# A third seven-product square in the last pair of an FFN block, and squares that wait for their parts one by one

## The reference

```python
def channel_mixer(h, up, conv_w, conv_b, down):
    hid = causal_dwconv(h @ up, conv_w, conv_b)      # 2048 -> 2 x 4096, convolution over 3 tokens
    gate, val = jnp.split(hid, 2, axis=-1)
    return (jax.nn.gelu(gate, approximate=True) * val) @ down   # 4096 -> 2048
```

## Time and profile before

| | |
|---|---|
| median of 3 runs | 3218.95 us (3218.23 to 3219.16) |
| the profiled execution's own time | 3219.05 us |
| its span in the trace | 3217.3 us |
| PE matmul busy | 3204.4 us, 100% of the span, 16261 matmuls |
| PE weight load busy | 2718.8 us, 85% |
| DVE busy | 2315.8 us, 72% |
| ACT busy | 1714.7 us, 53% |
| POOL busy | 183.0 us, 6% |
| chain that ended last | PE 99% of the span |
| DMA | 611.01 MB, mean 190 GB/s |
| granted TensorE clock | 0.999 in the mean |

### The profile page before, as it was taken

One profiled execution on the slowest core, in us unless ns is written; L12 is line 12 of the kernel. 1 busy time (PEld: TensorE's weight loads), 2 busy tenths in 40 slices (PEclk: granted clock), 3 DMA queues, 4 the chain that ended last, 5 costly groups with the idle time before them and its releaser, 6 DMA issues.

```text
span 3217.3 us, 42163 instructions
## 1 busy us (share of the span) xinstructions
PE 3204.4 (100%) x16261; PEld 2718.8 (85%) x16261; DVE 2315.8 (72%) x3007; ACT 1714.7 (53%) x2407; POOL 183.0 (6%) x194
## 2 busy tenths in 40 slices
PE   9999999999999999999999999999999999999999
PEld 7888888888888888888988888888888888888887
DVE  6576568767686877777565677877786667787777
ACT  6555545454554545455454565555565746555454
POOL 1033100010000000001000200000010020000001
PEclk9999999999999999999999999999999999999999
DMA  8945666665666666666656556666666545666665
GB/s 266 255 128 158 177 185 198 202 216 187 184 195 197 193 194 189 202 187 192 199 166 190 170 179 189 187 200 189 185 202 192 179 156 179 188 193 198 187 189 173
DMA packets 325452, 611.01 MB, mean 190 GB/s; under 512 B 19708, under 2 KB 47176, under 8 KB 324640
## 3 DMA queue, kind: packets, MB, share of 16 engines
q1 hardware_dynamic: 321776, 596.15, 60.9%
q0 software_dynamic: 3504, 12.52, 1.5%
HBM read 605.32 MB, written 3.28 MB: 189 GB/s over the span
## 4 chain that ended last, share of the span: by engine, by line
PE 99%; DMA 0%; ACT 0%; SPq 0%; DVE 0%; issue 0%; DVEq 0%; ACTq 0%
PE ps L546 21%; PE ps L387 16%; PE ps L389 16%; PE ps L388 16%; PE ps L549 11%; PE ps L398 2%; PE ps L400 2%; PE ps L399 2%; PE ps L534 2%; PE ps L532 2%; PE ps L533 2%; PE ps L726 1%; PE ps L750 1%; PE ps L621 1%; DMA raw<-w_in 0%; PE ps L715 0%
## 5 line engine op out<-in xcount | busy, mean ns | idle before, releaser
L373 DVE TENSOR_TENSOR w_lo<-raw,w_hi 128x1024 fp32r<-128x1024 f32 (+3 forms) x1041 | 1244.9, 1236 | 355.0 <-ACT w_hi L362 335.9
L362 ACT ACTIVATE w_hi<-raw 128x1024 fp32r<-128x1024 f32 (+3 forms) x1041 | 1041.4, 1039 | 395.5 <-DMA raw<-ffn_up 79.6
L546 PE MATMUL ps<-l_both,w_hi 128*128 128x512 f32 x2944 | 934.0, 396 | 0.0
L549 PEld LDWEIGHTS ps<-l_both,w_lo 128*128 128x128 f32 x2944 | 553.2, 188 | 122.4
L549 PE MATMUL ps<-l_both,w_lo 128*128 128x256 f32 x2944 | 594.4, 278 | 0.0
L546 PEld LDWEIGHTS ps<-l_both,w_hi 128*128 128x128 f32 x2944 | 456.1, 189 | 8.8
L387 PE MATMUL ps<-w_hi,m_hi 128*128 128x512 f32 (+1 forms) x1180 | 457.2, 387 | 0.0
L389 PE MATMUL ps<-w_hi,m_lo 128*128 128x512 f32 (+1 forms) x1180 | 454.6, 385 | 0.0
L388 PE MATMUL ps<-w_lo,m_hi 128*128 128x512 f32 (+1 forms) x1180 | 454.0, 385 | 0.0
L387 PE MATMUL ps<-w_hi,l_both 128*128 128x512 f32 (+3 forms) x1168 | 447.6, 383 | 0.7 <-DVE l_both L648 0.7
L389 PE MATMUL ps<-w_hi,l_both 128*128 128x512 f32 (+3 forms) x1168 | 440.4, 377 | 0.0
(11 more groups left out here) (633 smaller groups left out, 3499.1 us busy)
## 6 DMA issues: line engine op xcount, KB each, us to landing
raw<-ffn_up SPq DMA_DIRECT2D x256, 512.0 KB, 3.7
raw<-w_in SPq DMA_DIRECT2D x175, 512.0 KB, 3.7
raw<-w_mlp_in SPq DMA_DIRECT2D x128, 512.0 KB, 3.8
raw<-w_mlp_out SPq DMA_DIRECT2D x128, 512.0 KB, 4.3
raw<-ffn_down SPq DMA_DIRECT2D x128, 512.0 KB, 4.1
raw<-ab_w_in SPq DMA_DIRECT2D x64, 512.0 KB, 3.6
raw<-w_branch SPq DMA_DIRECT2D x48, 512.0 KB, 3.9
raw<-cd_w_in SPq DMA_DIRECT2D x40, 512.0 KB, 3.9
```

The costliest lines, as they stand in the source:

```text
L362: nc.scalar.activation(w_hi[:, k % RING, 0:n], raw[:, k % RING, 0:n], ACT.Copy).then_inc(hi_done, 1)
L373: nc.vector.tensor_tensor(w_lo[:, k % RING, 0:n], raw[:, k % RING, 0:n], w_hi[:, k % RING, 0:n].bitcast(F32), ALU.subtract).then_inc(lo_do ...
L546: return nc.tensor.matmul(ps[:, banks[t], :], hi[:, j, P * t:P * (t + 1)], l_both[:, kt, :], start=opens, stop=stop)
L549: return nc.tensor.matmul(ps[:, banks[t], 0:TOK], lo[:, j, P * t:P * (t + 1)], lh[0][:, kt, :], start=False, stop=stop)
```

## The change: what it does

1. In `quad`, the wait for both halves of the weight sums, which stood in front of the square, is split: the square starts with the three products that need no weight sum, then waits for the first half (t1, t3), and later for the second (t4, t2). This holds for all squares of the program.
2. The pair of g = 1 in both FFNs has three squares, at k = 4, 10 and 12, and takes its kt in natural order. So there are 50 squares instead of 48. The loads follow that order.
3. The activation sums of the third square come, as in g = 0, from `m_hi` + `m_lo` at the start of the pair's code; on DVE that code now waits for the last `hid_ready` itself.
4. The sums of the weights for the square at k = 10 get a `Part` of their own (`ffn_part_c`) in the room of `l_both` (`l_rows`), which the hidden steps no longer need.

```diff
@@ quad
             pe.wait_ge(s_lo_done, s + 1)
-            pe.wait_ge(t_lo_done, 2 * t + 2)
             pe.wait_ge(lo_done, 8 * q + k + 2)
...
             mm_tile(ps[:, cb, :], a12, b21, False, False)
             mm_tile(ps[:, cb + 2, :], n4, b22, False, False)
+            mm_tile(ps[:, mb, :], a11, b11, first, last)
+            pe.wait_ge(t_lo_done, 2 * t + 1)
+            mm_tile(ps[:, mb + 3, :], u1, t1, first, last)
+            mm_tile(ps[:, mb + 2, :], s3, t3, first, last)
+            pe.wait_ge(t_lo_done, 2 * t + 2)
             mm_tile(ps[:, cb + 1, :], a22, t4, False, False)
-            mm_tile(ps[:, mb, :], a11, b11, first, last)
-            mm_tile(ps[:, mb + 1, :], k1, t2, first, last)
-            mm_tile(ps[:, mb + 3, :], u1, t1, first, last)
-            mm_tile(ps[:, mb + 2, :], s3, t3, first, last).then_inc(chunk_used, 2)
+            mm_tile(ps[:, mb + 1, :], k1, t2, first, last).then_inc(chunk_used, 2)
@@ constants and buffers
+        F_LAST_QUADS, F_LAST_ORDER = (4, 10, 12), tuple(range(NCH))
...
-        ffn_parts = ((ffn_part, (ffn_part, ffn_part_b)), (ffn_part, (ffn_part_b, ffn_part)))
+        x_room = l_both[:, 0:8, :]
+        ffn_part_c = Part([l_rows[:, 0, 2 * BW * j:2 * BW * (j + 1)].rearrange("p (a b) -> p a b", a=2) for j in range(2)],
+                          [x_room[:, 4 + 2 * j:6 + 2 * j, :] for j in range(2)], [x_room[:, 2 * j:2 * j + 2, :] for j in range(2)])
+        ffn_parts = (ffn_part, (ffn_part, ffn_part_b), (ffn_part_c, ffn_part))
@@ SP: loads of the pair of g = 1
-                            load_block(sp, q + 20, down, D + 2 * P * F_ORDER[0][k // 2], BW * (k % 2), nch=1, k0=o + k)
+                            load_block(sp, q + 20, down, D + 2 * P * F_LAST_ORDER[k // 2], BW * (k % 2), nch=1, k0=o + k)
@@ ACT: the pairs
-                        if p == 0:
+                        if g == 0 and p == 0:
                             split_hi(act, x, range(o + 8, o + k))
...
                         else:
-                            quad_sums_hi(act, QS_F + 5 * layer + 2, ffn_sums, 2, ffn_s_raw)
+                            quad_sums_hi(act, QS_F + 6 * layer + 3 * g + 2, ffn_sums, 2, ffn_s_raw)
                             split_hi(act, x, (o + 8, o + 9))
-                            quad_hi(act, x, o + 10, QT_F + 7 * layer + 3, ffn_parts[layer][1])
-                            quad_hi(act, x, o + 12, QT_F + 7 * layer + 4, ffn_parts[layer][1])
+                            quad_hi(act, x, o + 10, QT_F + 8 * layer + 3 * g + 3, ffn_parts[1 + g])
+                            quad_hi(act, x, o + 12, QT_F + 8 * layer + 3 * g + 4, ffn_parts[1 + g])
@@ DVE: the pairs
-                        if p == 0:
+                        if g == 0 and p == 0:
                             split_lo(dve, x, range(o + 8, o + k))
...
                         else:
+                            dve.wait_ge(hid_ready, 8 * layer + 4 * g + 4)
                             for to, kt in ((ffn_a, F_THIRD), (ffn_b, F_THIRD + 1)):
                                 i = nc.vector.tensor_tensor(to, mh[0][:, kt, :].bitcast(F32), mh[1][:, kt, :].bitcast(F32), ALU.add)
                             chain(i)
-                            quad_sums(dve, QS_F + 5 * layer + 2, ffn_a, ffn_b, ffn_s_raw)
+                            quad_sums(dve, QS_F + 6 * layer + 3 * g + 2, ffn_a, ffn_b, ffn_s_raw)
                             split_lo(dve, x, (o + 8, o + 9))
...
```

More of the change, by code:

```diff
@@ L1634, in ffn @@
                     for p in range(2 - g):
-                        mm_pair(pe, q + 12 * g + 8 + 2 * p, o, u + 12 * g + 8 + 2 * p, p, mh, F_QUADS[p], QT_F + 7 * layer + 5 * g + 2 * p,
-                                QS_F + 5 * layer + 3 * g, ffn_sums, ffn_parts[layer][p], need=(hid_ready, h + 4 * g) if p == 0 else None, order=F_ORDER[p])
+                        mm_pair(pe, q + 12 * g + 8 + 2 * p, o, u + 12 * g + 8 + 2 * p, p, mh, F_LAST_QUADS if g else F_QUADS[p],
+                                QT_F + 8 * layer + 5 * g + 2 * p, QS_F + 6 * layer + 3 * g, ffn_sums, ffn_parts[2 * g + p],
+                                need=(hid_ready, h + 4 * g) if p == 0 else None, order=F_LAST_ORDER if g else F_ORDER[p])
                     for b in (2, 3) if g == 1 else ():
@@ L2119, in ffn @@
                             if b % 12 == 7:
-                                quad_hi(act, q + b, o + 12, QT_F + 7 * layer + 5 * g, ffn_part)
+                                quad_hi(act, q + b, o + 12, QT_F + 8 * layer + 5 * g, ffn_part)
                                 split_hi(act, q + b, (o + 14, o + 15))
@@ L2146, in ffn @@
                                     n = F_HID.index(j)
-                                    quad_sums_hi(act, QS_F + 5 * layer + 3 * g + n, ffn_sums, n, ffn_s_raw)
+                                    quad_sums_hi(act, QS_F + 6 * layer + 3 * g + n, ffn_sums, n, ffn_s_raw)
                     for p in range(2 - g):
@@ L2171, in ffn @@
                             split_hi(act, x, (o + 20, o + 21))
-                            quad_hi(act, x, o + 22, QT_F + 7 * layer + 2, ffn_part)
+                            quad_hi(act, x, o + 22, QT_F + 8 * layer + 2, ffn_part)
                         else:
@@ L2932, in ffn @@
                             if b % 12 == 7:
-                                quad_lo(dve, q + b, o + 12, QT_F + 7 * layer + 5 * g, ffn_part, 8)
+                                quad_lo(dve, q + b, o + 12, QT_F + 8 * layer + 5 * g, ffn_part, 8)
                                 split_lo(dve, q + b, (o + 14, o + 15))
@@ L2962, in ffn @@
                                 dve.wait_ge(conv_ready, n)
-                                quad_sums(dve, QS_F + 5 * layer + 3 * g + f, cg[:, F_TILE[f], :], cg[:, F_TILE[f] + 1, :], ffn_s_raw)
+                                quad_sums(dve, QS_F + 6 * layer + 3 * g + f, cg[:, F_TILE[f], :], cg[:, F_TILE[f] + 1, :], ffn_s_raw)
                             if val:
@@ L2968, in ffn @@
                             if summed:
-                                quad_sums_lo(dve, QS_F + 5 * layer + 3 * g + f, ffn_sums, f, ffn_s_raw)
+                                quad_sums_lo(dve, QS_F + 6 * layer + 3 * g + f, ffn_sums, f, ffn_s_raw)
                     for p in range(2 - g):
@@ L2972, in ffn @@
                         k = F_QUADS[p][-1]
-                        if p == 0:
+                        if g == 0 and p == 0:
                             split_lo(dve, x, range(o + 8, o + k))
-                            quad_lo(dve, x, o + k, QT_F + 7 * layer + 5 * g + 1, ffn_part, k - F_QUADS[p][0] - 2)
+                            quad_lo(dve, x, o + k, QT_F + 8 * layer + 1, ffn_part, k - F_QUADS[p][0] - 2)
                         else:
+                            dve.wait_ge(hid_ready, 8 * layer + 4 * g + 4)
                             for to, kt in ((ffn_a, F_THIRD), (ffn_b, F_THIRD + 1)):
@@ L3002, in ffn @@
                             split_lo(dve, x, (o + 20, o + 21))
-                            quad_lo(dve, x, o + 22, QT_F + 7 * layer + 2, ffn_part, 8)
+                            quad_lo(dve, x, o + 22, QT_F + 8 * layer + 2, ffn_part, 8)
                         else:
```

8 lines of the change are left out of this document (4 added, 4 removed).

## The result

The changed kernel takes 3230.54 us (median of 7 runs, 3228.43 to 3232.89), where the one before takes 3218.95 (7 runs, 3218.23 to 3219.61): a ratio of 1.0035 [1.0025, 1.0044], so 11.6 us slower. The prediction said 3231.0 us and +12.05. The profiled execution took 3230.74, its span is 3228.9.

The account below looks back on a forecast made before the run. PE was taken to bound the kernel, busy 100% of the span. Lateness of 6.64 and 6.97 us in the two layers, less 1.56 for the split wait, gave +12.05: 3231.0 us, range 3226.5 to 3236.

Parts of the forecast that it names:

- the saving: Pairs of g = 1: two squares replace two pairs of chunks, 4.85 us instead of 5.45 each, -1.20 us in all.
- the reading by the weight-load share: Skill's measure for PE: 85% occupied by weight loads, so removing matmuls might give nothing and the sum rise 1.2 us.
- nothing later takes it back: PE, whole kernel: every us PE is made to wait is lost, as PE has no idle time to absorb it.
- The split wait, -1.56: Second of two adjoining squares in the four MLP groups: the 0.39 us stall goes, 4 x 0.39 = -1.56 us.
- the new order of products costs nothing: All squares: same 21 matmuls and one more wait on a queue that runs ahead, so no cost.
- The rival that the split does nothing: Something else holds the second MLP square, so the split wait gains nothing: +13.6, 3232.6 us; chance 0.05.
- The chain at the start: Pair of g = 1: sums through DVE and ACT stall PE 3.4, 0.55, 1.7 us; 5.23 us late at k = 14.
- the prediction's own signs: Changed trace, both g = 1 pairs: PE idle about 3.4, 0.5, 1.7 us before k = 8, 10, 12; wrong if k = 12 under 1.
- the rival on the clock: TensorE's clock halves in the stalls: up to +18.3, 3237.2 us; small price 0.4 us likelier; chance 0.11 with lasting price.
- The end of the pair: Join 6.97 us late delays chunks 20 and 21; PE 6.64 us late in layer 0, 6.97 in layer 1.
- The rival that this end is hidden: Chunks 20 and 21: only 2 x 5.23 of lateness counts, +8.9, 3227.9 us; chance 0.14.
- Not slower: At `w_lo` of chunk 8, DVE's lead of 0.49 us hides the chain and the saving stays: 3216.3 us; chance 0.07.

Follow-up runs that it names:

- e9: Changed kernel with the third square's activation sums and the hi parts of chunks 20 and 21 made earlier, pair's first square at k = 2: 3215.75 us.
- e2: Changed kernel with the two waits put back as one ahead of each square, and the old order of products: 3235.63 us.
- e4: Changed kernel with ACT making the hi parts of chunks 20 and 21 ahead of its squares for the norm: 3227.55 us.
- e8: The changed kernel itself, run once more to look at the clock: 3229.03 us (one run).
- e10: Changed kernel with only the first square of the g = 1 pair moved from k = 4 to k = 2: 3219.15 us.
- e5: Changed kernel with earlier activation sums, earlier hi parts of chunks 20 and 21, and the last square at k = 14, not 12: 3227.55 us.
- e7: Changed kernel with chunks 8 and 9 split ahead of the third square's activation sums, on DVE and ACT: 3227.61 us.

## Why the prediction was right

**What bounds, and what is removed.** Right for the saving: where all waits are gone (e9), the square gives its 0.60 per layer to 0.1 us, so the reading by the weight-load share, by which it might give nothing, falls. Too strong in one sentence: "nothing later takes it back" holds only where no wait for DVE follows. In e2 PE comes 2.4 us later to k = 14 of layer 1, and segment 5 is the same to 0.03 us, since the later wait shrinks by as much.

**The split wait, -1.56.** Right in mechanism and in size: the four pairs of adjoining MLP squares are 0.38, 0.39, 0.43 and 0.38 us shorter than before, 1.57 in all. The MLP as a whole gives 1.86, since "the new order of products costs nothing" is not quite so: the stretches behind squares are 0.02 us shorter, fifteen times, while the program's first stretch of squares is 0.15 longer. Why, no run shows. The rival that the split does nothing falls.

**The chain at the start.** Forecast 3.4, 0.55 and 1.7 us in layer 0; measured 3.25, 0.51 and 1.64. Laying g = 0's rows over g = 1 gave DVE's list exactly. The term that was mis-sized is the lag between DVE's end and PE's start: I took 0.26 us from the earlier trace rows; at k = 8, 10 and 12 it is 0.15 (2347.94 + 1.22 = 2349.16, PE 2349.31). In layer 1 the stall at k = 10 is missing and the one at k = 12 is 0.90, since at half speed PE took longer over chunks 8 and 9; both layers reach k = 12 26.22 us after k = 4. As the prediction had it, how the stall is shared out doesn't matter. PE is 5.10 us late at k = 14 (31.15 us after k = 4, against 26.05), where I had 5.23. Two of the prediction's own signs did not come out in layer 1: a stall of about 0.5 at k = 10, and one of 1 us or more at k = 12, whose lack was named as a sign of being wrong. DVE's list is as forecast in both layers; in layer 1 slow matmuls fill a part of the time that PE would have waited, as the rival on the clock had it. The prediction's last part has a slip: 4.7 us is from the start of L2972 to `w_lo`, not from its end.

**The end of the pair.** The join is 6.95 us late (33.93 after k = 4, against 26.98), forecast 6.97. Behind it layer 0 is late by 6.30, not 6.64, and layer 1 by 7.60, not 6.97. The spread comes from POOL. The sum was right to 0.5 us partly by luck: segments 4 and 5 are 0.3 us more than forecast (13.9 against 13.6), segment 2 is 0.3 better, and these cancel. Of the waits at the end, forecast at about 0.7 and 0.6 us, the gaps show 0.43 and 0.50 in layer 0, 1.59 and 0.48 in layer 1. PE in both layers at k = 20 and 21 of the changed kernel (answers to the earlier trace rows):

```profile
2371.11 0.50 PE L387 MATMUL ps<-w_hi,m_hi 128*128 128x512 f32 x1 [0.27 <-DVE w_lo L373]
...
2374.47 0.50 PE L387 MATMUL ps<-w_hi,m_hi 128*128 128x512 f32 x1 [0.34 <-DVE w_lo L373]
```

```profile
3187.45 0.50 PE L387 MATMUL ps<-w_hi,m_hi 128*128 128x512 f32 x1 [1.43 <-DVE w_lo L373]
...
3190.80 0.50 PE L387 MATMUL ps<-w_hi,m_hi 128*128 128x512 f32 x1 [0.33 <-DVE w_lo L373]
```

DVE's split of chunk 20 in layer 0, in layer 1, and POOL's first multiplication in each (timelines of the changed kernel):

```profile
2369.12 1.94 DVE L373 TENSOR_TENSOR w_lo<-raw,w_hi 128x1024 fp32r<-128x1024 f32 x1 [3.58 <-ACT w_hi L362]
```

```profile
3184.28 3.11 DVE L373 TENSOR_TENSOR w_lo<-raw,w_hi 128x1024 fp32r<-128x1024 f32 x1 [3.58 <-ACT w_hi L362]
```

```profile
2367.58 5.75 POOL L1214 TENSOR_TENSOR main<-main 128x1024 f32<-128x1024 f32 x2 [7.08 <-ACT late L1741]
```

```profile
3183.91 5.75 POOL L1214 TENSOR_TENSOR main<-main 128x1024 f32<-128x1024 f32 x2 [8.25 <-DMA main<-ffn_post]
```

The same DVE instruction takes 1.94 us where POOL began 1.54 us ahead of it, 3.11 where POOL began 0.37 ahead; alone it takes 1.22. In both layers it ends 3.48 us after POOL's start. In layer 1 POOL had waited for its load, not for ACT. The rival that this end is hidden falls with e4, which took it away and gained.

**The clock.** It fell in one of the two long stalls of this execution, in layer 1 (stretches of the changed kernel, columns as in the earlier trace rows with the other engines between):

```profile
3148.36:3151.78 3.42, 0.35 (x2) 0.00 (x1) 1.78 (x5) 2.95 (x4) 0.00 (x0) 0.93 0.68 226
3151.78:3154.50 2.72, 2.69 (x6) 2.15 (x7) 2.72 (x3) 1.04 (x2) 0.00 (x0) 0.50 0.05 17
3154.50:3156.00 1.50, 1.50 (x8) 1.24 (x7) 1.43 (x4) 1.06 (x1) 0.00 (x0) 0.93 0.00 0
```

0.50 is 1.2 GHz, and matmuls start 0.43 us apart instead of 0.227. The rival's small price was the right one, and nearly nil: in the second profile (e8) the clock fell in both layers, and k = 12 came 26.72 and 26.23 us after k = 4, against 26.22 and 26.22. The later stalls for DVE swallow all but 0.5 us. The Trainium skill ("TensorE: Matmul & The Clock Gate", Part 1) says that idling throttles TensorE and activity releases it again; the trace agrees, since the speed came back while PE worked on.

**Not slower.** The lead of 0.49 us was as read; e10 shows the other side of that rival, a larger lead under which the same chain is free.

## What to carry to other kernels

Before an edit puts work on a helping engine, read how far that engine is ahead of PE at that place, not how idle it is on average (72% here): this change took 1.2 us of work from PE and cost it 15 in waits, restarts and slow matmuls (6.30 + 7.60 + 1.20) because DVE led by half a microsecond. The way out is not a shorter chain but a list in another order, with the chain ahead of the tight place and the load on DVE spread; and whoever moves the last product of a group later must ask who reads its accumulator and who waits for that (e5). Give an engine a wait for each operand where it is used: it was worth about 2 us alone, and 2.4 us of PE's place at k = 14 in each pair where squares adjoin.

## What the runs showed of the hardware that I had not expected

- The granted clock falls in some gaps and not in others of the same length. Past the first 20 us there are 14 gaps of 2.96 to 3.83 us between two matmul starts in these profiles (changed kernel 2, e8 2, e2 3, e4 2, e5 2, e7 2, e9 1 near its start). The clock fell to half speed in 11 of them or up to 1.3 us behind; of those from 0.7 to 2.03 us in none. In the changed kernel two gaps of 3.48 us differ in it. What decides, these runs don't tell.
- The scatter from run to run does not follow the stalls. The changed kernel's 7 runs spread over 4.5 us and the first 7 of before over 1.4, but the 20 to 27 runs of before in each later batch, which has no such stall, spread over 4.1 to 4.7, and the 9 of e4, with its stalls at k = 8, over 1.2.
- The lag from DVE's last write to PE's first matmul is not one number: 0.26 us behind the weight sums of before, 0.15 behind the splits at k = 8, 10 and 12, 0.06 behind a split that POOL ran beside (2370.98 + 3.43 = 2374.41, PE 2374.47), 0.05 behind the join in e5, where POOL did not run.
- Two plain elementwise instructions on DVE and POOL over 128x1024 f32 do not share the time in which they overlap: they take turns, and the one that began first keeps its length. POOL's first takes 2.40 us whether DVE's begins 0.37 or 1.54 us behind it, and DVE's ends 1.08 us after POOL's end both times, nearly as if it had begun there. Where DVE's began first, 0.47 us ahead (e4, layer 1), it kept its 1.22 and POOL's took 3.00. So DVE's takes 1.22 us alone and 1.43 (e8) to 3.43 behind POOL's, and a shift of 1.2 us in POOL's start moved PE's wait by 1.16 us (0.27 to 1.43).
